# The chunked RWKV-7 recurrence: the 64x64 inverse taken in 32x32 tiles, with the transposed copy made on VectorE

## What is computed

```python
def wkv_scan(r, w, k, v, a, b, s0, reverse):
    def step(S, xs):
        r_t, w_t, k_t, v_t, a_t, b_t = xs
        sa = jnp.einsum('bhvk,bhk->bhv', S, a_t)
        S = S * w_t[:, :, None, :] + sa[..., None] * b_t[:, :, None, :] + v_t[..., None] * k_t[:, :, None, :]
        return S, jnp.einsum('bhvk,bhk->bhv', S, r_t)
```

## Time and profile before

| what | value |
|---|---|
| median of 3 runs | 3419.12 us (3416.22 to 3426.52) |
| profiled execution, its own time | 3412.67 us |
| its span, first to last instruction | 3410.9 us |
| instructions | 72845 |
| TensorE busy, whole span | 2957.4 us, 87% |
| VectorE, ScalarE, GpSimd busy | 1448.0, 564.5, 377.9 us |
| mean granted TensorE clock | 0.929 of 2.4 GHz |
| the changed block, about | from 1030 us to 1820 us of the span |

### The profile page before, as it was taken

One profiled execution on the slowest core, in us unless ns is written; L12 is line 12 of the kernel. 1 busy time (PEld: TensorE's weight loads), 2 busy tenths in 40 slices (PEclk: granted clock), 3 DMA queues, 4 the chain that ended last, 5 costly groups with the idle time before them and its releaser, 6 DMA issues. The chain is left out here.

```text
span 3410.9 us, 72845 instructions
## 1 busy us (share of the span) xinstructions
PE 2957.4 (87%) x32237; PEld 1759.9 (52%) x32237; DVE 1448.0 (42%) x2634; ACT 564.5 (17%) x1331; POOL 377.9 (11%) x431
## 2 busy tenths in 40 slices
PE   5899999998595888888884499977999999999993
PEld 1566666665375888888882245442333333323230
DVE  1677577663363665565652311142232232132123
ACT  2100000000352333333332311110000000000001
POOL 0100000000154232322211000000000000000000
PEclk8899999999597999999995799978999999999996
DMA  9565645552451000000005387777999999999997
GB/s 412 195 213 175 208 176 183 208 196 84 143 132 46 24 5 26 26 26 26 25 8 229 138 300 289 276 308 283 395 410 393 412 412 395 399 397 400 408 419 309
DMA packets 224486, 776.86 MB, mean 228 GB/s; under 512 B 55171, under 2 KB 119386, under 8 KB 155635
## 3 DMA queue, kind: packets, MB, share of 16 engines
q1 hardware_dynamic: 212626, 712.26, 54.1%
q0 software_dynamic: 11248, 60.87, 5.9%
q10 hardware_dynamic: 368, 0.10, 0.0%
HBM read 710.98 MB, written 62.18 MB: 227 GB/s over the span
## 5 line engine op out<-in xcount | busy, mean ns | idle before, releaser
L2068 PE MATMUL ex_ps<-experts_ring,ex_xe 128*32 128x512 f32 (+1 forms) x4608 | 674.6, 599 | 49.1 <-DMA experts_ring<-in_w_up 27.6
L2070 PE MATMUL ex_ps<-experts_ring,ex_xe 128*32 128x512 f32 (+1 forms) x1536 | 674.1, 599 | 0.0
L2068 PEld LDWEIGHTS ex_ps<-experts_ring,ex_xe 128*32 128x32 f32 (+1 forms) x4608 | 212.6, 107 | 497.0 <-issue 479.4
L474 DVE SCALAR_TENSOR_TENSOR pj_macc<-pj_mring,head_cond_t,pj_macc 128x1024 f32<-128x1024 f32 x240 | 296.9, 1277 | 184.0 <-DMA pj_mring<-in_w_ada 184.0
L2083 PE MATMUL ex_ps<-experts_ring,ex_hidt 128*32 128x512 f32 (+1 forms) x2304 | 334.3, 594 | 6.9 <-DVE ex_hidt L2150 6.9
L2085 PE MATMUL ex_ps<-experts_ring,ex_hidt 128*32 128x512 f32 (+1 forms) x768 | 333.8, 594 | 0.0
L547 PE MATMUL pj_ps<-head_hT,head_ring_in 128*128 128x320 f32 x1104 | 313.7, 437 | 5.9 <-DVE head_hT L447 3.5
L1866 PE MATMUL om_ps<-experts_ring,om_ot 128*128 128x512 f32 x640 | 287.1, 610 | 15.4 <-DMA om_ot<-scratch_o 15.4
L2172 DVE SCALAR_TENSOR_TENSOR ex_hid<-ex_hid,ex_gcol,ex_ps 80x512 f32<-80x512 f32 x16 | 11.9, 744 | 591.3 <-ACT ex_hid L2115 591.3
L547 PEld LDWEIGHTS pj_ps<-head_hT,head_ring_in 128*128 128x128 f32 x1104 | 211.4, 192 | 96.6 <-DVE head_hT L447 6.3
L2083 PEld LDWEIGHTS ex_ps<-experts_ring,ex_hidt 128*32 128x32 f32 (+1 forms) x2304 | 106.8, 106 | 225.9 <-issue 218.1
(11 more groups left out here) (357 smaller groups left out, 4417.4 us busy)
## 6 DMA issues: line engine op xcount, KB each, us to landing
experts_ring<-in_w_gate SPq DMA_DIRECT2D x128, 1024.0 KB, 21.9
experts_ring<-in_w_up SPq DMA_DIRECT2D x128, 1024.0 KB, 22.6
experts_ring<-in_w_down SPq DMA_DIRECT2D x128, 1024.0 KB, 21.3
experts_ring<-in_w_out SPq DMA_DIRECT2D x68, 1024.0 KB, 6.9
pj_mring<-in_w_ada SPq DMA_DIRECT2D x64, 1024.0 KB, 9.0
head_ring_in<-in_w_in SPq DMA_DIRECT2D x23, 2048.0 KB, 8.0
ada_ring<-in_w_ada SPq DMA_DIRECT2D x16, 2048.0 KB, 19.0
scratch_z<-pj_stage POOLq DMA_DIRECT2D x19, 640.0 KB, 8.2
```

Of the source, the lines that this page charges most:

```text
L474: a = nc.vector.scalar_tensor_tensor(acc, w, scalar, acc, ALU.mult, ALU.add)
L2068: pe.matmul(ps[rows, bank, :], xe[:, k, rows], cols, start=(k == 0), stop=(k == KD - 1))
L2070: mm = pe.matmul(ps[96:96 + rows.stop - rows.start, bank, :], xe[:, k, rows], up[:, g1], start=(k == 0), stop=(k == KD - 1))
```

## The change

The inverse is taken in 32x32 tiles. The two diagonal 32x32 blocks of every 64x64 matrix are inverted first (levels 0 to 3), four tiles (two heads, two blocks) side by side on partitions 0, 32, 64 and 96; `tt` and `tm` hold these blocks only. Level 4, the last, makes the off-diagonal block. `tw` holds the whole inverse for the chain; GpSimd writes its diagonal blocks (`spread_own`) and VectorE the other one. A level has two products, `x` and `d`. `tm` is no longer updated on TensorE: after each `d` VectorE transposes `tt` into `tm` in 32x32 blocks (`turn`). `dt` and `ti` are gone. Chunks go in two batches of five.

The plan is ordered anew, and a planner (`COST`) spreads the 30 stages of the chain over it. `sc` comes first in a period, each with a `w` or `a` job of the next unit behind it; `bk`, `s0` and `vt` fill places between the levels. `vt` is made once per pair and not per unit. `rot` has four banks, and `wu` and `zo` have one more each; `bk`, `aq`, `ec` and others have more buffers. `st` is now made by a tensor_tensor with a product of two decays that GpSimd prepares (`decay_pairs`). The exponentials stand apart and not in one row. `CHAINS` = 1: one chain at a time, as before. The order of an odd period that it gives (turn, scan, exp and pad are VectorE's and ScalarE's own items):

```diff
-    LEVELS = [2, 4, 8, 16, 32]
-    BATCH = [(0, 4), (4, 7), (7, 10)]
...
-    R = 6
...
+    CHAINS = 1
+    R = 4
+    NU = 2 * NPAIR
+    NS = 1 + CHAINS
+    HB, BC = CK // 2, NCK // 2
+    LAST_LV = 4
...
-    plan = [("bk", b) for b in range(3)] + [("vt", b) for b in range(2)] + [("sc", b) for b in range(NCK // 2)]
-    plan += FRONT_JOBS + [("ti", b) for b in range(3)]
-    for level in range(len(LEVELS)):
-        plan += [("x", b, level) for b in range(3)]
-        for b in range(3):
-            plan += [("dt", b, level)] if level < len(LEVELS) - 1 else []
-            plan += [("dtt", b, level)]
...
+    GROUPS = tuple(slice(HB * g, HB * g + HB) for g in range(4))
...
+    def front_jobs(v):
+        return [("w", 0, v), ("w", 1, v), ("a", 0, v), ("a", 1, v), ("s0", 0, v)] if v < NU else []
+
+    def plan(u):
+
+        fr = front_jobs(u + 1) + [None] * 5
+        vt = [("vt", b, u) for b in range(2)] if u % 2 == 0 else [None] * 2
+        more = u + 1 < NU
+        items = [("sc", 0, u), fr[0], ("sc", 1, u), fr[1], ("sc", 2, u), fr[2], ("sc", 3, u), fr[3], ("sc", 4, u)]
+        items += ["scan"] if more else []
+        fill = [("bk", 0, u), ("bk", 1, u), ("bk", 2, u), fr[4], vt[0], vt[1]]
+        for lv in range(LAST_LV + 1):
+            for b in range(2):
+                items += (["turn%d" % b] if lv == 0 else []) + [("x", b, lv, u)]
+            if lv < 3:
+                items.append(fill[2 * lv])
+            for b in range(2):
+                items.append(("d", b, lv, u))
+                if more and lv == 3:
+                    items.append(("exp_in", "exp_inv")[b])
+                if more and lv == 4:
+                    items += (["pad_b"], ["pad_k", "pad_a"])[b]
+            if lv < 3:
+                items.append(fill[2 * lv + 1])
+            if more and lv == 3:
+                items += ["exp_ex", "decay"]
+        return [i for i in items if i is not None]
+
+    def chain(v, i0, i1):
+        return [("seq", v, i, s) for i in range(i0, i1) for s in ("pw", "u", "z")] if 0 <= v < NU else []
+
+    def sequence(u):
+        if CHAINS == 1:
+            return chain(u - 1, 0, NCK)
+        old, new = chain(u - 2, BC, NCK), chain(u - 1, 0, BC)
+        return [s for pair in itertools.zip_longest(old, new) for s in pair if s is not None]
+
+    COST = {"sc": 9, "w": 6, "a": 6, "s0": 2, "bk": 9, "vt": 6, "x": 7, "d": 7}
+
+    def timeline(u):
+
+        items, seq = plan(u) if u < NU else [], sequence(u)
+        total = sum(COST[i[0]] for i in items if not isinstance(i, str))
+        out, spent, placed = [], 0, 0
+        for i in items:
+            out.append(i)
+            spent += 0 if isinstance(i, str) else COST[i[0]]
+            while placed < len(seq) and (placed + 1) * total <= spent * len(seq):
+                out.append(seq[placed])
+                placed += 1
+        return out + seq[placed:]
+
+    LINES = [timeline(u) for u in range(NU + CHAINS)]
...
+    def on_act(key):
+        return key[0] in ("w", "a", "s0", "vt", "bk") or key[0:1] + key[2:3] == ("x", LAST_LV)
...
             ch.link(nc.gpsimd.memset(join[:], 1.0))
-            for i in range(6):
+            for i in range(5):
                 n = 2 ** i
-                for rows in HEADS:
+                for rows in GROUPS:
...
+            for g, rows in enumerate(GROUPS):
+                for h in range(2):
+                    ch.link(nc.gpsimd.memset(half[rows, h:h + 1], 1.0 if h == g % 2 else 0.0))
+            for h in range(2):
+                ch.link(nc.gpsimd.tensor_scalar(first[:, h, :], join[:, 0, :], half[:, h:h + 1], None, ALU.mult))
+            assert ch.n == MADE, ch.n
...
+            def start(u, b):
+
+                n = MADE + 3 * (2 * u + b)
+                pool.wait_ge(dve_ev, RANK[G["sc", (BC * b + BC - 1) // 2, u]])
+                lt = chunks(sc[:, u % NS, :, 0, 0:CK], b).rearrange("p c (h k) -> p c h k", k=HB)
+                nc.gpsimd.tensor_tensor(part[:], lt, first[:].unsqueeze(1).to_broadcast([P, BC, 2, HB]), ALU.mult).then_inc(tinit, 1)
+                pool.wait_ge(tinit, n + 1)
+                nc.gpsimd.tensor_tensor(chunks(tt, b), part[:, :, 0, :], part[:, :, 1, :], ALU.add).then_inc(tinit, 1)
+                pool.wait_ge(tinit, n + 2)
+                nc.gpsimd.tensor_tensor(chunks(tt, b), chunks(tt, b), eye32[:].unsqueeze(1).to_broadcast([P, BC, HB]), ALU.add).then_inc(tinit, 1)
+
+            def spread_own(u, b):
+
+                d = u % 2
+                pool.wait_ge(dve_ev, RANK[G["d", b, LAST_LV - 1, u]])
+                nc.gpsimd.tensor_scalar(chunks(tw[:, u % NS, :, HB * d:HB * d + HB], b), chunks(tt, b), half[:, d:d + 1], None, ALU.mult).then_inc(spread, 1)
+
...
-                    for i, c in enumerate(range(*BATCH[b])):
-                        lhs, rhs = {"x": (sc[:, d, c, 0, 0:CK], tm[:, c, :]), "dt": (tt[:, d, c, :], xm[:, c, :]),
-                                    "dtt": (xm[:, c, :], tt[:, d, c, :])}[kind]
-                        mm = heads(bank[:, i * CK:(i + 1) * CK], lhs, rhs, True, True)
+                    last = key[2] == LAST_LV
+                    for i in range(BC):
+                        c = BC * b + i
+                        out = bank[:, i * HB:(i + 1) * HB]
+                        for g, rows in enumerate(GROUPS):
+                            at = GROUPS[g ^ 1] if last else rows
+                            if kind == "x":
+                                h = (g + 1) % 2 if last else g % 2
+                                lhs, rhs = sc[rows, u % NS, c, 0, HB * h:HB * h + HB], tm[rows, c, :]
+                            else:
+                                lhs, rhs = xm[rows, c, :], tt[rows, c, :]
+                            mm = pe.matmul(out[at], lhs, rhs, start=True, stop=True)
...
+            def turn(u, b):
+                nc.vector.transpose(chunks(tm, b).rearrange("p c k -> p (c k)"), chunks(tt, b).rearrange("p c k -> p (c k)")).then_inc(turned, 1)
...
+                lv = key[2]
+                src = bank[:, 0:BC * HB].rearrange("p (c k) -> p c k", k=HB)
+                if kind == "x":
+                    nc.vector.tensor_tensor(chunks(xm, b), src, join[:, lv + 1:lv + 2, :].to_broadcast([P, BC, HB]), ALU.mult).then_inc(dve_ev, 1)
+                elif lv < LAST_LV:
+                    nc.vector.tensor_tensor(chunks(tt, b), src, chunks(tt, b), ALU.add).then_inc(dve_ev, 1)
+                    dve.wait_ge(dve_ev, RANK[G[key]])
+                    turn(u, b)
                 else:
-                    lv = plan[n][2]
-                    c0, c1 = BATCH[b]
-                    src = bank[:, 0:(c1 - c0) * CK].rearrange("p (c k) -> p c k", k=CK)
-                    if kind == "x":
-                        a = nc.vector.tensor_tensor(xm[:, c0:c1, :], src, join[:, lv + 1:lv + 2, :].to_broadcast([P, c1 - c0, CK]), ALU.mult)
-                    else:
-                        t = tm[:, c0:c1, :] if kind == "dt" else tt[:, d, c0:c1, :]
-                        a = nc.vector.tensor_tensor(t, src, t, ALU.add)
+                    h = 1 - d
+                    nc.vector.scalar_tensor_tensor(chunks(tw[:, u % NS, :, HB * h:HB * h + HB], b), chunks(tt, b), half[:, h:h + 1], src,
+                                                   ALU.mult, ALU.add).then_inc(dve_ev, 1)
...
-                    nc.vector.tensor_scalar(st[:], tmp[:], ec[:, d, c:c + 1], ec[:, d, nx:nx + 1],
-                                            ALU.mult, ALU.mult).then_inc(s_ready, 1)
+                    nc.vector.tensor_tensor(st[:, k, :], tmp[:, k, :], ecp[:, r, c:c + 1].to_broadcast([P, DH]), ALU.mult).then_inc(s_ready[k], 1)
```

More of the change, by code:

```diff
@@ new lines, in _ @@
+            pool.wait_ge(once_in, 8 * 16)
+            front(0)
+            scaled_r(0)
+            decay_pairs(0)
+            added = 0
+            for u in range(NU):
+                for b in range(2):
+                    start(u, b)
+                if u + 1 < NU:
+                    front(u + 1)
+                    scaled_r(u + 1)
+                for b in range(2):
+                    spread_own(u, b)
+                if u + 1 < NU:
+                    decay_pairs(u + 1)
+                if u % 2 == 0 and u // 2 >= CHAINS:
+                    add_directions(added)
+                    added += 1
@@ L1379, in period @@
-            def period(p, d, first, last):
-                for item in timeline:
-                    if item[0] == "job":
-                        run_job(item[1], p, d, first, last)
-                    elif not first:
-                        stage(item[1], item[2], 2 * p + d - 1, 1 - d)
-            pe.wait_ge(loads, NLOAD)
-            for n, (kind, half) in enumerate(FRONT_JOBS):
-                front_job(kind, half, 0, rot[:, n]).then_inc(job, 1)
-            periods(period)
-            for i, s in stages:
-                stage(i, s, 2 * NPAIR - 1, 1)
+                    pe.wait_ge(w_ev[k], q + 1)
@@ L1483, in _ @@
-            copy_values(0)
```

(31 more changed lines are left out.)

552 lines of the change are left out of this document (255 added, 297 removed).

## The result

The changed kernel takes 3598.73 us (median of 4 runs, 3595.27 to 3612.64) against 3419.67 us for the kernel before (4 runs, 3416.22 to 3426.52): ratio 1.0529 [1.0495, 1.0562]. The prediction had the sign (slower) and not the size: 3598.73 lies above the range's end of 3560.

A forecast was written before the change was run, and what follows sets the result against it. TensorE's own in-order queue was taken to bound the kernel; a period of 49.0 us for 45.8 gave +48 over fifteen, edges +6, so 3467 to 3473, said as 3470 us; 8-in-10 range 3375 to 3560.

The forecast's parts named there:

- Records: TensorE's x and d jobs: 17.5 ns a record, 0.70 us a job, 14.0 us a period for 17.5 before.
- The clock: TensorE's clock in the block: stays at 0.95 or more, since its gaps are no longer than before.
- The sum again: One period: 34.2 issue, 10.0 waits and 4.8 tile changes make 49.0 us, 3.2 more than 45.8.
- Waits on VectorE: TensorE's waits on VectorE and ScalarE: 10.0 us a period, with X00 2.7, X10 1.1 and SC0 for aq 2.7.
- Changes of tile: TensorE between 32x32 and 64x64 jobs: 0.15 us each, 30 a period, 4.5 us, plus some 0.3 of small chain waits.
- What costs nothing: VectorE's emptying and ten transposes, GpSimd's work under the levels, four banks for six, early loads: no added time.
- Edges: Mask building, first period and last chain, outside the fifteen periods: together +6 us.
- The fixed time per record: Rival on small-tile pace: 29.1 ns a record, 1.16 us a job, period 57.3, about 3598 us; chance 0.2.
- Fast tiles: Rival on small-tile pace: 7.9 ns a record, 0.32 us a job, period 42.7, about 3379 us; chance 0.27.
- the middle that was taken: The forecast itself on small-tile pace: 13 to 22 ns a record, with drains, 3440 to 3510 us; chance 0.42.
- No drain: Rival on tile changes between 64x64 and 32x32: they cost nothing, period 45.1, 3415 us, no change; chance 0.1.
- The chain as the floor: Rival on the period: the chain alone limits it, so nothing moves; rejected at about 27 us a period; no own chance.

The follow-up runs named there:

- Where the order has no wait over 1.9 us: Changed kernel with two bk jobs ahead of the first sc and the cumulative sum behind the second x job: 3502 us, ratio 1.0250.
- half the tiles: Changed kernel with bk jobs first, cumulative sum later, two chains, and two of four tiles in levels 0 to 3, inverse left out: 3408 us.
- the filled waits: Changed kernel with two unread 512-column products ahead of the waits of each unit's first sc and first x job: 3524 us, ratio 1.0321.
- Both runs in which records were left out: Two of four tiles in levels 0 to 3: on the changed kernel 3505 us; with bk first, cumulative sum later and two chains 3408 us.
- the run made for it: Changed kernel with 640 records of 32x32 and then 640 of 64x64 added behind the block, without waits between them: 3637 us.

## Why the prediction was wrong, by its own steps

*Records.* The step took 17.5 ns, the middle of 7.9 and 29.1, and 0.70 us a job. Measured 9.5 ns and 0.38 us of the job's own at the high clock (0.48 less the 0.10 of the change). The 0.70 looks right only at the low level, where a job with its change takes 0.68 (1390.25 to 1390.93). The sum was 20 x 0.32 = 6.4 us a period too high here.

*What the step left out.* It priced a record by what TensorE does with it, and not by how it gets there. On average the supply would do: 1312 records in a period of 49 us are 128 every 4.8 us, and it brings them every 3.4 to 4.2. But the jobs of 0.48 us stand close together in the second half of a period, and there 127 records are used up in 2.8 us (1437.06 to 1439.86). That is worth 2.9 us a period in waits so marked. The kernel before has 1135 records a period, 64-wide or more, and shows next to none (0.5 us in all). No row ahead of the prediction showed a gap of this kind.

*The clock.* "The clock should stay at 0.95 or more, since TensorE's gaps are no longer than before." This is the step that failed: the forecast put the low clock at nothing, and it fell to 0.76, with 27.5 us of a period at the low level. The premise on the gaps was wrong by the forecast's own waits: it had 2.7 and 1.1 us for `tm` and 2.7 for `aq`, where the longest in eight periods of before was 1.9. And it was too narrow. Where the order has no wait over 1.9 us the clock is still 0.77, and with half the tiles it falls without a wait, too (both above).

The price can be read off the groups at both levels: four records of 64 columns stand 0.12 and 0.22 us apart, 16 of 128 columns 0.88 and 1.76, a `w` or `a` job 0.73 and 1.36, a job of small tiles takes 0.48 and 0.69. So a record loses 25, 55, 315 and 5 ns. Of the fifteen periods some 2450, 700, 60 and 4000 such records are at the low level, which makes 9.3 us a period, and 0.7 before. This is an estimate. It bears the check of the filled waits: priced in the same way that run loses 4.2 us a period, 5.1 less, and its period fell by 4.3.

*The sum again.* 49.0 less 6.4 for the records, 2.9 more for the supply and 9.3 for the clock are 54.8, against the measured 56.2. The rest is about in the waits: idle time apart from the gaps at `rot` grew by 3.6 us a period (11.8 less 2.9, against 5.3), where the forecast had 1.6 more (10.0 against 8.4). Up to 1.3 us of it, at `zo` and `wu`, have no cause in the trace and may in part be the supply's too.

The sign was luck. With the measured 9.5 ns a record the forecast's own sum is 42.6 us a period, 3.2 less than before, or some 3377 us: faster. The kernel is slower by the clock and the supply, which the sum had at nothing.

*Waits on VectorE.* Right in place and near in size: X00 2.7 forecast and 2.30 in the trace, X10 1.1 and 0.84 to 1.06, `aq` 2.7 and 2.8 on average. The average hides two sizes, 2.1 and 3.5, told below. The forecast's wait of 1.9 us in the exponentials did not come; they stand far enough apart, and the longest wait for `usb` is 1.1. Those on `st` are 0.7 where 0.8 was said.

*Changes of tile.* 0.15 us each, as said. The trace shows it at single places; 30 of them a period as a sum was not tested apart.

*What costs nothing.* VectorE's transposes take 343 ns, 0.33 was said, and VectorE is busy 21.8 us of a period, less than before. Right, but for its last product, told below.

*Edges.* +6 said, +28 and +5 found. The masks were right. The groups of GpSimd after have their selects of 32 columns in two lines; the first is:

```profile
L1263 POOL TENSOR_SCALAR_AFFINE_SELECT rw_join<-rw_join 32x32 f32<-32x32 f32 x20 | 5.6, 280 | 1.4
```

That is the 0.28 us that was said, and from its first MEMSET to its last mask GpSimd takes 4.6 us more, for 4.5. The first product comes 10.8 us later, for 5.4: 4.1 us stand ahead of the block, 1.2 more pass up to the first cumulative sum, and the wait for `aq` is the 0.9 that was said. The first period was thought 1 us longer and is 17: its clock is 0.57, where it had 0.94, and it has 6.8 us of causeless waits and 3.8 for `tm`.

*The rivals.* The fixed time per record gave 3598 us and the kernel takes 3598.73. That is chance: its job of 1.16 us is nowhere in the trace, and it had no loss of clock. What it had right is that a long stream of records has a price of 27 to 31 ns. Fast tiles was nearest on the pace (7.9 ns for 9.5) and is 220 us off, since it had neither the supply nor the clock. Its condition (under 13 ns) held; it had been given 0.27, and the middle that was taken 0.42. No drain is refuted by the 0.15. The chain as the floor stays without support.

*How the 10.4 us of a period divide*, as far as the rows go: +8.6 for the clock (9.3 less 0.7, the estimate above), +2.9 for gaps of the supply at `rot`, +3.6 for other idle time, and -4.7 for TensorE's own work at the high level (the busy time grew by 3.9). Clock and supply are not independent: the gaps can bring the clock down too (1385.20).

*Still open.* What brings the clock down, in shares. Filling two waits shows that waits have a part; the kernel with two chains and half the tiles shows falls without them. Both runs in which records were left out have 0.76 to 0.78.

## What to carry to other kernels

Smaller tiles side by side make records cheap in columns, but each is still an instruction. Before a change that raises their number, count the records of the densest stretch and compare with what the trace has shown to arrive, here 128 every 3.4 to 4.2 us. And when a forecast of a TensorE-bound stage has a new wait, or many narrow products that no row of the profile has, don't take the clock from the profile before: give the low level a price of its own, from groups that stand at both levels.

## What was unexpected of the hardware

- The program reaches TensorE in pieces of 128 records, at best one every 3.4 to 4.2 us, with some 246 records ready at the start of the run made for it. Emptied, the store shows as idle time with no cause, in the middle of a group of like instructions.
- Behind a single gap of 1.82 us the clock was at the low level for some 30 us, with TensorE at work for most of it and one wait of 2.12 us in it. And it fell at 1218.48 of the run with two chains and half the tiles with no wait ahead of it, behind 6.9 us in which TensorE was busy for 6.8.
- VectorE's last product of a period takes 0.82 us in one period and 2.15 in the next, when GpSimd sums the directions. The timeline of all engines after:

```profile
1343.47 0.82 DVE L1589 TENSOR_TENSOR rw_bk<-rw_kd,rw_e_inv 128x640 f32<-128x640 f32 x1
...
1343.87 1.82 POOL L1330 TENSOR_TENSOR rw_osum<-rw_of 128x640 f32<-128x640 f32 x1 [4.31 <-issue]
1344.21 2.15 DVE L1593 SCALAR_TENSOR_TENSOR rw_aq<-rw_kk,rw_e_ex 128x640 f32<-128x640 f32 x1
...
1346.62 1.97 PE L1368 MATMUL rw_rot<-rw_aq,rw_bk 64*64 64x128 f32 x16 [3.46 <-DVE rw_aq L1593]
```

  The product ends 0.67 us behind the end of GpSimd's, so it got hardly anything done beside it. This makes the wait for `aq` 3.46 us in such a period and 2.12 in the other. The Trainium skill ("SBUF — State Buffer", SBUF: two separate sides) has a rule for it: a VectorE operation with two inputs in SBUF and a GpSimd one that reads SBUF share a port as an exclusive lock, and the later one stands still. The trace agrees in these 1.33 us. Moving the sum was not tried.
